# Scan stage of a hybrid SSD / attention layer: two elementwise steps per block formed by GpSimd instead of VectorE

## The chip, the cores and the metric

The kernel runs on one core of one Trainium2 chip, in one launch. The metric is the device time of that core in microseconds. The core has five engines with queues of their own: TensorE (PE in the profile; PEld is its weight load), VectorE (DVE), ScalarE (ACT), GpSimd (POOL) and SyncE (SP, which here issues DMAs). They wait for each other through semaphores only.

## The reference, cut to what matters

The model has two layers. Each layer mixes tokens by two groups of heads, a bidirectional state-space scan (SSD) and a latent attention, and then runs a feed-forward part (dense in layer 0, routed experts in layer 1). There are 512 latent tokens and 128 context tokens, that is five blocks of 128 tokens, which the scan treats as chunks. What the change touches is the scan's output:

```python
decay = jnp.exp(jnp.where(lower, seg, -jnp.inf))
scores = jnp.einsum('bcthn,bcshn->bctsh', cc, bc) * decay * dtc[:, :, None, :, :]
y_intra = jnp.einsum('bctsh,bcshp->bcthp', scores, xc)
...
y_inter = jnp.einsum('bcthn,bchpn->bcthp', cc, h_start) * jnp.exp(la)[..., None]
...
y_ssd = y_f + flip(y_b) + d_skip[:, None] * xs
y_ssd = y_ssd * jax.nn.silu(z)
```

The forward and the backward scan share B, C and x inside a chunk, so their decay matrices (each with its dt folded in) can be added first and multiplied by the shared C.B scores once.

## The kernel before, in words

`Mixer.run` calls, once per layer, `stage_in_proj`, `stage_ssd`, `stage_attention` and `stage_out_proj`. Each stage is one block of code per engine; all engines meet at a barrier at its end. Nothing reorders instructions: each engine runs the list that its function writes, and waits where the code says so.

`stage_in_proj` matters here for what its trace shows. GpSimd subtracts a rounded weight piece from the raw one (`split_lo`, L621, two inputs in SBUF, 128x2048 or 128x2752 elements), while VectorE runs the convolution (L737 and L739) on tiles in SBUF and copies results out of PSUM (L728 to L731).

`stage_ssd` first prepares (state, chunk states, the C.B scores `cbs`), then runs a loop over five blocks b = 0 to 4, the last of them the context. In the loop, with the lines of the profile:

- TensorE, block b: the inter-chunk product (L994, not for b = 4), then the decay exponents of block b+1 for both directions (L947, L949: `every_la`), then steps of the modulation matrix product that rides along (`mod`: L204 turns a finished row, L216 multiplies the next unit; a unit's L216 waits until VectorE has taken the unit before it), then y (L1007: scores times x, 16 records per block), which waits for the scores and for VectorE to be done with the y of the block before, and then the block's remaining modulation steps. After y of block 4 come the last unit (L216) and its turning.
- ScalarE, block b: the exponentials of block b+1 (L878: eight per direction, written to `seg`, which has two rooms, so it waits for y of block b-1), the copy of the modulation row (L242), and squares of the latents (L901, L903).
- VectorE, block b: adds the two directions' decays in place (L1114, 128x1024: the sum), multiplies by `cbs` (L1118: the multiply, which releases y on TensorE), forms d_skip times x (L1119, 128x512: the skip product, into t3), scales the inter-chunk product out of PSUM (L1124, twice), adds it up (L1127, L1128), takes a finished modulation unit (L232 out of PSUM, L234 from two SBUF tiles; L234 releases the next L216), waits for y, adds it (L1132) and multiplies by z (L1133, which counts `y_used`). In block 0 a second unit is taken (L232, L234) after L1133. In block 4 VectorE first waits for all squares (L1111, L1112).
- GpSimd has no code in this stage.

The stage ends with the last unit: L216, the row on ScalarE (L242), its turning, L232 and L234, and a reciprocal (L1138). SyncE loads the modulation weights ahead through eight rooms; these DMAs are idle in the last microseconds of the stage.

Of the kernel before, what the change touches and what calls it, by code (L numbers as in the profile page):

```python
# [16 lines left out]
ALU = mybir.AluOpType  # L17
# [3 lines left out]
P = 128  # L21
# [5 lines left out]
TB = T // P  # L27
LB = LAT // P
HT = T // 2
SEQ_OF = [0] * LB + [1]  # L30
SSDW, NH, HD, NG, NS = 512, 8, 64, 2, 64
# [47 lines left out]
def insert_dim(ap, at, n):  # L79

    dims = [list(d) for d in ap.ap]
    dims.insert(at, [0, n])
    return bass.AP(tensor=ap.tensor, offset=ap.offset, ap=dims)


class Program:
# [36 lines left out]
    def sb(self, name, shape, dt=F32, ctx=None):  # L123
        return (ctx or self.ctx).enter_context(self.nc.sbuf_tensor(name, shape, dt))
# [25 lines left out]
def chained(signal):  # L150

    count = [0]

    def link(eng, ins):
        count[0] += 1
        ins.then_inc(*signal.up())
        eng.wait_ge(*signal.at(count[0]))
    return link
# [594 lines left out]
def stage_ssd(p, l, t):  # L753

    nc, io = p.nc, p.io
    small, st_in = p.sig("ssd_small_ahead"), p.sig("ssd_state_ahead")
# [6 lines left out]
    st_turned, st_kept, turned, xst_dve, xst_act, btok_out = (p.sig(n) for n in (  # L763
        "ssd_st_turned", "ssd_st_kept", "ssd_turned", "ssd_xst_dve", "ssd_xst_act", "ssd_btok_out"))
# [4 lines left out]
    lab_ps, dec_ready, s_ready, inter_ps, inter_used, y_ps, y_used = (p.sig(n) for n in (  # L769
        "ssd_lab_ps", "ssd_decay", "ssd_scores", "ssd_inter_ps", "ssd_inter_used", "ssd_y_ps", "ssd_y_used"))  # L770
    squares, parts_ready = p.sig("pn_squares"), p.sig("silu_parts_ready")
    ahead_in, lat_mean, lat_root = p.sig("at_ahead_in"), p.sig("at_mean"), p.sig("at_root")
    with ExitStack() as own:
        def sb(name, shape):
            return p.sb(f"ssd_{name}{l}", shape, ctx=own)
# [24 lines left out]
        junk, junk2 = sb("junk", [P, QR]), sb("junk2", [P, KVR])  # L800
        cbs = sb("cbs", [P, NG, TB, P])
        t1, t2, t3 = sb("t1", [P, SSDW]), sb("t2", [P, SSDW]), sb("t3", [P, SSDW])
        seg = t["qkv_room"][:, 0:4 * NH * P].rearrange("p (r d h c) -> p r d h c", r=2, d=2, h=NH)
        xbc, z, xst, y = t["xbc"], t["z"], t["xst"], t["y_ssd"]
        dtb, alog, dsk, stl = t["dt_bias"], t["a_log"], t["d_skip"], t["stl"]
# [4 lines left out]
        act_blocks = (1, 2, 4)  # L810
# [3 lines left out]
        def mod_steps(slot):  # L814

            return [UNIT_STEPS * int(item[1]) + s for item in plan[slot]
                    for s in (range(MM_STEPS) if item[0] == "m" else (MM_STEPS,))]
# [5 lines left out]
        def by_block(tile):  # L823
            return tile.rearrange("p d b h -> p b d h")

        with nc.Block() as block:
            @block.sync
            def _(sp):
                mod.load(sp)
                sp.dma_start(t["past"], io["cache_ckv"][0, l]).then_inc(*ahead_in.up(16))  # L830
                sp.dma_start(t["kvrow"], io["kv_norm"][l].partition_broadcast(P)).then_inc(*ahead_in.up(16))
                sp.dma_start(t["cos"], io["rope_cos"].rearrange("(b p) r -> p b r", p=P)).then_inc(*ahead_in.up(16))
                sp.dma_start(t["sin"], io["rope_sin"].rearrange("(b p) r -> p b r", p=P)).then_inc(*ahead_in.up(16))
                sp.wait_ge(*fin_out.at(1))
                for d in range(2):
                    for g in range(2):
                        sp.dma_start(io["new_ssm"][0, l, d, 4 * g:4 * g + 4].rearrange("(j h) q n -> (h q) j n", h=2),
                                     stl[:, d, :, g * NS:(g + 1) * NS]).then_inc(*fin_stored.up(16))
                sp.wait_ge(*fin_stored.at(64))
# [174 lines left out]
            def _(dve):  # L1014
                link = chained(dve_c)
# [81 lines left out]
                def by_group(ap):  # L1097
                    return ap.rearrange("p (g h q) -> p g h q", g=NG, q=HD)

                def inter(d):  # L1100
                    return p.psum[:, 5:7, d * 256:(d + 1) * 256].rearrange("p g (h q) -> p g h q", q=HD)

                def heads(ap):
                    return ap.rearrange("p (h q) -> p h q", h=NH)
                dve.wait_ge(*scanned.at(1))
                for b in range(TB):
                    f, r = seg[:, b % 2, 0], seg[:, b % 2, 1]
                    if b == TB - 1:
                        dve.wait_ge(*squares.at(2 * TB))
                        stat = t["stat"]  # L1110
                        dve.tensor_scalar(stat[:, 0], stat[:, 0], 1.0 / QR, EPS, ALU.mult, ALU.add)  # L1111
                        dve.tensor_scalar(stat[:, 1], stat[:, 1], 1.0 / KVR, EPS, ALU.mult, ALU.add).then_inc(*lat_mean.up())  # L1112
                    dve.wait_ge(*dec_ready.at(2 * b + 2))
                    link(dve, dve.tensor_tensor(f, f, r, ALU.add))  # L1114
                    if b == 0:
                        dve.wait_ge(*cb_kept.at(1))
                    grouped = f.rearrange("p (g h) c -> p g h c", g=NG)
                    dve.tensor_tensor(grouped, grouped, insert_dim(cbs[:, :, b], 2, NH // NG), ALU.mult).then_inc(*s_ready.up())  # L1118
                    link(dve, dve.tensor_tensor(heads(t3[:]), heads(xst[:, b]), dsk[:].to_broadcast([P, NH, HD]), ALU.mult))  # L1119
                    if b < LB:  # L1120
                        dve.wait_ge(*inter_ps.at(b + 1))
                        for d, out in enumerate((t1, t2)):
                            grown = el[:, d, b].rearrange("p (g h) -> p g h", g=NG).to_broadcast([P, NG, NH // NG, HD])
                            ins = dve.tensor_tensor(by_group(out[:]), inter(d), grown, ALU.mult)  # L1124
                        ins.then_inc(*inter_used.up())
                        dve.wait_ge(*inter_used.at(b + 1))
                        link(dve, dve.tensor_tensor(t1[:], t1[:], t2[:], ALU.add))  # L1127
                        link(dve, dve.tensor_tensor(t3[:], t3[:], t1[:], ALU.add))  # L1128
                    for step in mod_steps(2 * b):
                        mod.on_vector(dve, step)  # L1130
                    dve.wait_ge(*y_ps.at(b + 1))
                    link(dve, dve.tensor_tensor(t3[:], t3[:], p.psum[:, 4], ALU.add))  # L1132
                    dve.tensor_tensor(y[:, b], t3[:], z[:, b], ALU.mult).then_inc(*y_used.up())  # L1133
                    dve.wait_ge(*y_used.at(b + 1))
                    for step in mod_steps(2 * b + 1):
                        mod.on_vector(dve, step)
# [1865 lines left out]
class Mixer:  # L3002
# [31 lines left out]
    def run(self, h, slots, ahead, r=None):  # L3034
        p, l, t = self.p, self.l, self.t
        p.silu_wide = t["silu_wide"]
        stage_in_proj(p, l, self.weights, h[:, 0], h[:, 1], t)
        self.inner.close()
        stage_ssd(p, l, t)
        self.scan.close()  # L3040
        stage_attention(p, l, t, slots)
        self.last = stage_out_proj(p, l, t, h, ahead, r)
        self.mixer.close()
# [146 lines left out]
```

## Time and profile before

| | us |
|---|---|
| median of 3 runs | 2041.09 (2039.52 to 2041.40) |
| span of the profiled execution, first to last instruction | 2035.5 |
| scan loop, layer 0 (first L1114 to the end of the last L1133) | 187.40 to 232.36 |
| scan loop, layer 1 (first L1114 to the end of the last L1133) | 1081.86 to 1126.96 |
| GpSimd busy, whole span | 98.2 in 64 instructions |
| VectorE busy, whole span | 1296.3 |

The profiled execution has no separate whole time in the list of times: what is known of it is its span, which is 5.6 us under the median. In the timeline a row gives start, length, engine, line, operation, the tile written <- the tiles read, the form, the count, and in brackets how long the engine stood idle before it and what ended that. A row with a count over one merges neighbours of the same line, and its length runs from the first start to the last end.

### The profile page before, as it was taken

The page shows a single profiled execution, that of the slowest core. Times are in us where ns is not written, and L with a number is a line of the kernel's source. Part 1 is how long each engine was busy: PE and PEld are TensorE (multiplying, and loading weights), DVE is VectorE, ACT ScalarE, POOL GpSimd, SP SyncE. Part 2 cuts the span into 40 slices and gives each one's busy share as a digit, 9 for nine tenths or more (in the row PEclk, how much of TensorE's full clock was granted, in tenths as well). Part 3 has the DMA queues.
Part 4 walks back from the last instruction along what each step waited for, and adds up shares of the span by engine and source line. Part 5 has one row for each costly group of instructions (what it writes and reads, how often), then busy time and mean ns, then how long its engine had stood idle before and what let it go on. Part 6 is the DMA issues. An engine that isn't in the chain of part 4 may idle for free. (4 is left out here: it accounts for less than half of the span.)

```text
span 2035.5 us, 31746 instructions
## 1 busy us (share of the span) xinstructions
PE 1909.9 (94%) x11144; PEld 1615.2 (79%) x11144; DVE 1296.3 (64%) x1973; ACT 1087.1 (53%) x1785; POOL 98.2 (5%) x64
## 2 busy tenths in 40 slices
PE   5997799899999999998988899889999999999998
PEld 2995575599998998997985665887888888888885
DVE  3835766574323333356817666657888888888888
ACT  4225654454211211235226554547888888888885
POOL 0330000000000000000400000002000000000002
PEclk9999899899999999998999899899999999999999
DMA  6204512202223213212216601149978191918395
GB/s 261 98 27 176 209 69 104 102 3 84 68 84 98 73 55 94 81 52 90 76 72 230 255 22 42 64 153 383 410 283 321 60 358 43 362 60 322 109 324 188
DMA packets 132849, 303.41 MB, mean 149 GB/s; under 512 B 20496, under 2 KB 66448, under 8 KB 129680
## 3 DMA queue, kind: packets, MB, share of 16 engines
q1 hardware_dynamic: 126608, 279.51, 37.9%
q10 hardware_dynamic: 3264, 12.07, 1.5%
q0 software_dynamic: 2880, 10.49, 1.4%
q8 instruction: 67, 1.10, 0.2%
q14 instruction: 30, 0.25, 0.0%
HBM read 360.43 MB, written 28.10 MB: 191 GB/s over the span
## 5 line engine op out<-in xcount | busy, mean ns | idle before, releaser
L2587 DVE TENSOR_TENSOR ex_wl<-ex_raw,ex_wh 128x1024 fp32r<-128x1024 f32 x351 | 418.8, 1220 | 25.6 <-ACT ex_wh L2426 14.3
L2426 ACT ACTIVATE ex_wh<-ex_raw 128x1024 fp32r<-128x1024 f32 x351 | 367.8, 1060 | 71.1 <-PE psum L2506 45.2
L2832 PE MATMUL psum<-norm_out,ex_w_hi 128*128 128x320 f32 x1408 | 267.7, 308 | 2.6 <-PEq L1771 2.6
L2506 PE MATMUL psum<-ex_wh,ex_he_hi 128*128 128x512 f32 (+1 forms) x624 | 242.2, 388 | 2.4 <-DVE ex_he_lo L2559 1.2
L2506 PE MATMUL psum<-ex_wl,ex_he_hi 128*128 128x512 f32 (+1 forms) x624 | 233.2, 374 | 0.1
L2506 PE MATMUL psum<-ex_wh,ex_he_lo 128*128 128x512 f32 (+1 forms) x624 | 232.9, 373 | 0.0
L2832 PEld LDWEIGHTS psum<-norm_out,ex_w_hi 128*128 128x128 f32 x1408 | 222.0, 187 | 3.0 <-DVE ex_w_lo L2693 2.8
L2693 DVE TENSOR_TENSOR ex_w_lo<-side,ex_w_hi 128x1024 fp32r<-128x1024 f32 (+1 forms) x82 | 82.6, 1014 | 166.3 <-ACT ex_w_hi L2689 166.0
L2832 PE MATMUL psum<-norm_out,ex_w_lo 128*128 128x320 f32 x704 | 165.2, 308 | 0.0
L2767 ACT ACTIVATE ex_sg_hf<-psum 128x640 f32<-128x640 f32 x22 | 15.5, 706 | 235.4 <-PE psum L2832 235.4
L2506 PEld LDWEIGHTS psum<-ex_wh,ex_he_hi 128*128 128x128 f32 x624 | 117.9, 189 | 25.0 <-issue 6.3
L2506 PEld LDWEIGHTS psum<-ex_wh,ex_he_lo 128*128 128x128 f32 x624 | 118.2, 189 | 22.2 <-issue 3.2
L2506 PEld LDWEIGHTS psum<-ex_wl,ex_he_hi 128*128 128x128 f32 x624 | 118.0, 189 | 20.9
L708 PE MATMUL psum<-win_hi,norm_out 128*128 128x256 f32 (+1 forms) x640 | 133.1, 300 | 0.1
L2689 ACT ACTIVATE ex_w_hi<-side 128x1024 fp32r<-128x1024 f32 (+1 forms) x82 | 70.5, 888 | 98.6 <-DMA side<-ffn_w_down 61.5
L2832 PEld LDWEIGHTS psum<-norm_out,ex_w_lo 128*128 128x128 f32 x704 | 118.7, 187 | 0.0
L708 PEld LDWEIGHTS psum<-win_hi,norm_out 128*128 128x128 f32 x640 | 104.7, 188 | 0.4 <-POOL win_lo L621 0.4
L2525 PE MATMUL psum<-ex_wh,ex_hh 128*128 128x512 f32 x260 | 104.7, 403 | 0.0
L2587 DVE TENSOR_TENSOR ex_wl<-x,ex_wh 128x1024 fp32r<-128x1024 f32 x65 | 77.2, 1220 | 38.6 <-ACT ex_wh L2426 38.6
L2525 PE MATMUL psum<-ex_wl,ex_hh 128*128 128x512 f32 x260 | 101.6, 391 | 0.0
L2525 PE MATMUL psum<-ex_wh,ex_hl 128*128 128x512 f32 x260 | 101.5, 390 | 0.0
L1513 PE MATMUL psum<-mx_qkv_room,at_qT 96*128 96x320 f32 (+3 forms) x320 | 92.6, 413 | 6.5 <-ACT at_items_room L1392 5.0
(462 smaller groups left out, 3903.7 us busy)
## 6 DMA issues: line engine op xcount, KB each, us to landing
ex_raw<-moe_gate_up SPq DMA_DIRECT2D x221, 512.0 KB
ex_raw<-moe_w_down SPq DMA_DIRECT2D x143, 512.0 KB
x<-moe_gate_up SPq DMA_DIRECT2D x64, 512.0 KB
wmod_ssd<-w_mod SPq DMA_DIRECT2D x56, 512.0 KB, 6.2
wmod_at<-w_mod SPq DMA_DIRECT2D x24, 512.0 KB, 4.1
side<-ffn_w_gate SPq DMA_DIRECT2D x22, 512.0 KB, 3.9
side<-ffn_w_up SPq DMA_DIRECT2D x22, 512.0 KB, 3.9
mx_qkv_room<-w_in SPq DMA_DIRECT2D x10, 1024.0 KB, 4.9
```

Of the source, the lines that this page charges most:

```text
L708: last = pe.matmul(p.psum[:, bank_of(g), 0:width], mh[:, k, j * P:(j + 1) * P], mw[:, k, :], start=(k == 0 and n == 0), stop=(k == KD - 1 ...
L1513: last = pe.matmul(p.psum[:, 2 * (n % 2) + part, 0:w], qT[0:rows, h, b * P:(b + 1) * P], kT[0:rows, h, lo + part * w:lo + (part + 1) * w], ...
L2426: act.activation(wh[:, i % RING], raw_of(i), ACT.Copy).then_inc(*hi_done.up(1))
L2506: last = pe.matmul(p.psum[:, 2 + g % 2, 0:width], h[:, k], w[:, i % RING, cols], start=(k == 0 and m == 0), stop=(k == KD - 1 and m == 2))
L2525: last = pe.matmul(p.psum[:, half], h[:, f], w[:, i % RING, cols], start=(f == 0 and m == 0), stop=False)
L2587: dve.tensor_tensor(wl[:, i % RING], raw_of(i), wh[:, i % RING].bitcast(F32), ALU.subtract).then_inc(*lo_done.up(1))
L2689: act.activation(self.wh[:, i % self.RING, part], self.room[:, i % 2, part], ACT.Copy).then_inc(self.hi_done, 1)
L2693: dve.tensor_tensor(self.wl[:, i % self.RING, part], self.room[:, i % 2, part], self.wh[:, i % self.RING, part].bitcast(F32), ALU.subtract ...
L2767: act.activation(sg.rearrange("p (a c) -> p a c", a=2), halves_of(home[i]), ACT.Silu).then_inc(*gate_act.up())
L2832: last = pe.matmul(p.psum[:, home[i] + half, 0:HT], m[:, i % w.RING, cols], x[:, k, half * HT:(half + 1) * HT], start=(k == 0 and n == 0), ...
```

## The change

The code of the scan's loop is split over two engines. GpSimd gets a function in this stage: per block it forms the skip product into a new tile `skip` with two rooms (d_skip times x, 128x512) and then, when the exponentials of both directions are there, the sum in place (128x1024). Its first skip product stands before the loop; the product of block b+1 stands in its list directly behind the sum of block b, and from block 2 on it waits until VectorE has finished the block two before. VectorE loses L1114 and L1119; its multiply waits for GpSimd's sum (`both_summed`), and its L1128 reads `skip`. Besides, the semaphores of the input projection are given back for reuse before the scan.

```diff
         t1, t2, t3 = sb("t1", [P, SSDW]), sb("t2", [P, SSDW]), sb("t3", [P, SSDW])
+        skip = sb("skip", [P, 2, SSDW])
...
+            @block.gpsimd
+            def _(pool):
+                pool.wait_ge(*small.at(0))
+                pool.wait_ge(*xst_dve.at(2))
+                pool.wait_ge(*xst_act.at(len(act_blocks)))
+                for b in range(TB):
+                    if b >= 2:
+                        pool.wait_ge(*y_used.at(b - 1))
+                    pool.tensor_tensor(heads(skip[:, b % 2]), heads(xst[:, b]), dsk[:].to_broadcast([P, NH, HD]),
+                                       ALU.mult).then_inc(*skip_ready.up())
+                    pool.wait_ge(*dec_ready.at(2 * b + 2))
+                    pool.tensor_tensor(seg[:, b % 2, 0], seg[:, b % 2, 0], seg[:, b % 2, 1],
+                                       ALU.add).then_inc(*both_summed.up())
...
-                    dve.wait_ge(*dec_ready.at(2 * b + 2))
-                    link(dve, dve.tensor_tensor(f, f, r, ALU.add))
+                    dve.wait_ge(*both_summed.at(b + 1))
...
-                    link(dve, dve.tensor_tensor(heads(t3[:]), heads(xst[:, b]), dsk[:].to_broadcast([P, NH, HD]), ALU.mult))
...
-                        link(dve, dve.tensor_tensor(t3[:], t3[:], t1[:], ALU.add))
+                        dve.wait_ge(*skip_ready.at(b + 1))
+                        link(dve, dve.tensor_tensor(t3[:], skip[:, b % 2], t1[:], ALU.add))
...
-                    link(dve, dve.tensor_tensor(t3[:], t3[:], p.psum[:, 4], ALU.add))
+                    if b == LB:
+                        dve.wait_ge(*skip_ready.at(b + 1))
+                    link(dve, dve.tensor_tensor(t3[:], t3[:] if b < LB else skip[:, b % 2], p.psum[:, 4], ALU.add))
...
+        for prefix in ("win_", "conv_"):
+            p.retire(prefix)
```

On VectorE, block 0 of the loop in layer 0 before (`mx_qkv_room` is `seg`, `halves` is x or y, `modsums` the modulation unit):

```order
L1114 TENSOR_TENSOR mx_qkv_room0<-mx_qkv_room0 128x1024 [waits ssd_decay,ssd_scanned]
L1118 TENSOR_TENSOR mx_qkv_room0<-mx_qkv_room0,ssd_cbs0 128x1024 [waits ssd_cb_kept,dve_chain]
L1119 TENSOR_TENSOR ssd_t30<-halves,mx_d_skip0 128x512
L1124 TENSOR_TENSOR ssd_t10<-psum,ssd_ect0 128x512 [waits ssd_inter_ps,dve_chain]
L1124 TENSOR_TENSOR ssd_t20<-psum,ssd_ect0 128x512
L1127 TENSOR_TENSOR ssd_t10<-ssd_t10,ssd_t20 128x512 [waits ssd_inter_used]
L1128 TENSOR_TENSOR ssd_t30<-ssd_t30,ssd_t10 128x512 [waits dve_chain]
L232 TENSOR_REDUCE modsums_ssd0<-psum 128x8 [waits mod_turned,dve_chain]
L234 TENSOR_TENSOR mod<-modsums_ssd0,vectors_sb 128x8 [waits mod_summed]
L1132 TENSOR_TENSOR ssd_t30<-ssd_t30,psum 128x512 [waits ssd_y_ps]
L1133 TENSOR_TENSOR halves<-ssd_t30,halves 128x512 [waits dve_chain]
```

The same place after the change, whose line numbers are those of the changed file:

```order
L1134 TENSOR_TENSOR mx_qkv_room0<-mx_qkv_room0,ssd_cbs0 128x1024 [waits ssd_cb_kept,ssd_both_summed,ssd_scanned]
L1139 TENSOR_TENSOR ssd_t10<-psum,ssd_ect0 128x512 [waits ssd_inter_ps]
L1139 TENSOR_TENSOR ssd_t20<-psum,ssd_ect0 128x512
L1142 TENSOR_TENSOR ssd_t10<-ssd_t10,ssd_t20 128x512 [waits ssd_inter_used]
L1144 TENSOR_TENSOR ssd_t30<-ssd_skip0,ssd_t10 128x512 [waits ssd_skip,dve_chain]
L232 TENSOR_REDUCE modsums_ssd0<-psum 128x8 [waits mod_turned,dve_chain]
L234 TENSOR_TENSOR mod<-modsums_ssd0,vectors_sb 128x8 [waits mod_summed]
L1150 TENSOR_TENSOR ssd_t30<-ssd_t30,psum 128x512 [waits ssd_y_ps]
L1151 TENSOR_TENSOR halves<-ssd_t30,halves 128x512 [waits dve_chain]
```

The sum and the skip product are gone from VectorE's list, the multiply stands first and waits for `ssd_both_summed`, and the second addition waits for `ssd_skip`; all else keeps its place.

On GpSimd, from the last weight pieces of the input projection of layer 0 to the attention stage, before:

```order
L621 TENSOR_TENSOR win_lo0<-mx_qkv_room0,win_hi0 128x2752 [waits win_hi_done] x2
L621 TENSOR_TENSOR win_lo0<-mx_qkv_room0,win_hi0 128x2048 [waits win_hi_done] x2
L650 UNCONDITIONAL_BRANCH
L1276 UNCONDITIONAL_BRANCH [waits barrier_Pool_Activation_PE_DVE_SP_gather]
L1278 MEMSET at_krt0 128x576
```

The same place after the change:

```order
L650 UNCONDITIONAL_BRANCH
L832 UNCONDITIONAL_BRANCH [waits barrier_Pool_Activation_PE_DVE_SP_gather]
L840 TENSOR_TENSOR ssd_skip0<-halves,mx_d_skip0 128x512 [waits ssd_xst_act,ssd_xst_dve,pool_chain]
L843 TENSOR_TENSOR mx_qkv_room0<-mx_qkv_room0 128x1024 [waits ssd_decay]
L840 TENSOR_TENSOR ssd_skip0<-halves,mx_d_skip0 128x512
L843 TENSOR_TENSOR mx_qkv_room0<-mx_qkv_room0 128x1024 [waits ssd_decay]
L840 TENSOR_TENSOR ssd_skip0<-halves,mx_d_skip0 128x512 [waits ssd_y_used]
L843 TENSOR_TENSOR mx_qkv_room0<-mx_qkv_room0 128x1024 [waits ssd_decay]
...
L831 UNCONDITIONAL_BRANCH
```

Ten instructions per layer stand there that were not there; the second skip product follows the first sum without any wait, the later ones wait for `ssd_y_used`.

## Rows read from the trace of the kernel before

**Rows 1.** The page, its first line.

```profile
span 2035.5 us, 31746 instructions
```

**Rows 2.** Timeline of VectorE in the scan of layer 0.

```profile
187.40 1.23 DVE L1114 TENSOR_TENSOR mx_qkv_room<-mx_qkv_room 128x1024 f32<-128x1024 f32 x1 [2.87 <-ACT mx_qkv_room L878]
188.66 1.22 DVE L1118 TENSOR_TENSOR mx_qkv_room<-mx_qkv_room,ssd_cbs 128x1024 f32<-128x1024 f32 x1
189.80 0.68 DVE L1119 TENSOR_TENSOR ssd_t<-halves,mx_d_skip 128x512 f32<-128x512 f32 x1
...
192.57 0.69 DVE L1128 TENSOR_TENSOR ssd_t<-ssd_t 128x512 f32<-128x512 f32 x1
...
193.52 0.17 DVE L234 TENSOR_TENSOR mod<-modsums_ssd,vectors_sb 128x8 f32<-128x8 f32 x1
...
199.30 0.17 DVE L234 TENSOR_TENSOR mod<-modsums_ssd,vectors_sb 128x8 f32<-128x8 f32 x1
...
209.49 1.22 DVE L1118 TENSOR_TENSOR mx_qkv_room<-mx_qkv_room,ssd_cbs 128x1024 f32<-128x1024 f32 x1
...
214.35 0.17 DVE L234 TENSOR_TENSOR mod<-modsums_ssd,vectors_sb 128x8 f32<-128x8 f32 x1
...
225.80 0.17 DVE L1111 TENSOR_SCALAR mx_stat<-mx_stat 128x5 f32<-128x5 f32 x1 [2.32 <-ACT ssd_junk L903]
...
227.20 1.22 DVE L1118 TENSOR_TENSOR mx_qkv_room<-mx_qkv_room,ssd_cbs 128x1024 f32<-128x1024 f32 x1
```

**Rows 3.** Timeline of TensorE in the scan of layer 0.

```profile
193.74 1.92 PE L216 MATMUL psum<-wmod_ssd,silu_wide 128*32 128x512 f32 x16 [2.33 <-DVE mod L234]
...
204.85 1.90 PE L1007 MATMUL psum<-halves,mx_qkv_room 128*128 128x64 f32 x16
...
228.48 2.43 PE L1007 MATMUL psum<-halves,mx_qkv_room 128*128 128x64 f32 x16 [2.97 <-DVE mx_qkv_room L1118]
230.84 3.12 PE L216 MATMUL psum<-wmod_ssd,silu_wide 128*32 128x512 f32 x16
```

**Rows 4.** Timeline of ScalarE in the scan of layer 0.

```profile
185.13 2.17 ACT L878 ACTIVATE mx_qkv_room<-psum,ssd_bias 128x128 f32<-128x128 f32 x8
...
190.08 4.23 ACT L878 ACTIVATE mx_qkv_room<-psum,ssd_bias 128x128 f32<-128x128 f32 x16 [1.60 <-PE psum L949]
...
203.74 4.23 ACT L878 ACTIVATE mx_qkv_room<-psum,ssd_bias 128x128 f32<-128x128 f32 x16 [1.63 <-PE psum L949]
```

**Rows 5.** Timeline of GpSimd in the input projection of layer 0.

```profile
74.56 4.60 POOL L621 TENSOR_TENSOR win_lo<-mx_qkv_room,win_hi 128x2048 fp32r<-128x2048 f32 x1 [6.99 <-ACT win_hi L617]
...
105.50 6.70 POOL L621 TENSOR_TENSOR win_lo<-mx_qkv_room,win_hi 128x2752 fp32r<-128x2752 f32 x1 [9.37 <-ACT win_hi L617]
```

**Rows 6.** Timeline of VectorE in the same stretch, in two narrow windows.

```profile
74.56 5.28 DVE L739 SCALAR_TENSOR_TENSOR conv_acc<-conv_pad,vectors_sb,conv_acc 128x644 f32<-128x644 f32 x1
...
105.31 7.58 DVE L739 SCALAR_TENSOR_TENSOR conv_acc<-conv_pad,vectors_sb,conv_acc 128x644 f32<-128x644 f32 x2
```

**Rows 7.** Line L739: count, then shortest, median and longest duration in ns.

```profile
L739 DVE SCALAR_TENSOR_TENSOR conv_acc<-conv_pad,vectors_sb,conv_acc x48: 887/890/6656, 68.0 to 1000.7; 128x644 f32<-128x644 f32 x48
```

**Rows 8.** Groups of GpSimd by form: busy us, mean ns of one, idle before.

```profile
L621 POOL TENSOR_TENSOR win_lo<-mx_qkv_room,win_hi 128x2048 fp32r<-128x2048 f32 x8 | 36.8, 4603 | 56.6 <-ACT win_hi L617 56.6
...
L2054 POOL TENSOR_TENSOR rt_strict<-tri,ident 128x128 f32<-128x128 f32 x1 | 0.5, 453 | 0.0
```

**Rows 9.** Timeline of GpSimd at the start: two neighbours without a wait.

```profile
2.15 0.28 POOL L302 TENSOR_SCALAR_AFFINE_SELECT tri<-tri 128x128 f32<-128x128 f32 x1
2.40 0.28 POOL L304 TENSOR_SCALAR_AFFINE_SELECT tri<-tri 128x128 f32<-128x128 f32 x1
```

**Rows 10.** Windows: start:end, length, busy us (x instructions) per engine, PEclk, DMA share, GB/s.

```profile
231.00:234.00 3.00, 2.96 (x16) 0.44 (x12) 1.33 (x2) 0.00 (x0) 0.00 (x0) 0.62 0.00 0
```

**Rows 11.** Timeline of VectorE, first sum in the scan of layer 1.

```profile
1081.86 1.22 DVE L1114 TENSOR_TENSOR mx_qkv_room<-mx_qkv_room 128x1024 f32<-128x1024 f32 x1 [2.87 <-ACT mx_qkv_room L878]
```

More of the change, by code:

```diff
@@ L771, in stage_ssd @@
     squares, parts_ready = p.sig("pn_squares"), p.sig("silu_parts_ready")
+    both_summed, skip_ready = p.sig("ssd_both_summed"), p.sig("ssd_skip")
     ahead_in, lat_mean, lat_root = p.sig("at_ahead_in"), p.sig("at_mean"), p.sig("at_root")
@@ L824, in by_block, with heads @@
             return tile.rearrange("p d b h -> p b d h")
+        def heads(ap):
+            return ap.rearrange("p (h q) -> p h q", h=NH)
         with nc.Block() as block:
+            @block.gpsimd
[11 more added lines that the diff above has]
+                                       ALU.add).then_inc(*both_summed.up())
             @block.sync
@@ L1101, in inter @@
                     return p.psum[:, 5:7, d * 256:(d + 1) * 256].rearrange("p g (h q) -> p g h q", q=HD)
-                def heads(ap):
-                    return ap.rearrange("p (h q) -> p h q", h=NH)
                 dve.wait_ge(*scanned.at(1))
                 for b in range(TB):
-                    f, r = seg[:, b % 2, 0], seg[:, b % 2, 1]
+                    f = seg[:, b % 2, 0]
                     if b == TB - 1:
```

## The prediction

> **What bounds the kernel now.** I read the page first, then the timelines of VectorE, TensorE and ScalarE over the scan of layer 0, and then those of GpSimd and VectorE over the input projection, because only there does the trace show GpSimd at elementwise work. The span is 2035.5 us [rows 1]; the change touches two loops of some 45 us each. The loop of layer 1 begins with the same 2.87 us of idle time before the same sum [rows 2, 11], so I work out layer 0 and count it twice.
>
> In the loop three engines hand work round. The first sum starts when ScalarE's exponentials end (185.13 + 2.17 = 187.30, sum at 187.40) [rows 2, 4]; the multiply follows, then VectorE works down to L234 at 193.52 to 193.69, and only then does TensorE's next unit start, at 193.74, after 2.33 us of idle time that L234 ended [rows 2, 3]. Behind that unit stand y of block 0, the next inter-chunk product and the exponents of block 2. So L234 sets the pace, and all that stands ahead of it on VectorE counts. In block 4 it is otherwise: VectorE waits for the squares until 225.80, its multiply ends at 227.20 + 1.22 = 228.42, and TensorE, 2.97 us idle, starts y(4) at 228.48 [rows 2, 3]. From there the last unit, its row and its turning follow in a line to the barrier, so **the start of y(4) is the quantity to work out**: what it moves by, the end moves by. Later stages load their data only once they are reached, so nothing absorbs it.
>
> **What the change removes.** Per block one sum of 1.23 us and one skip product of 0.68 us on VectorE [rows 2], 1.9 us with no cover on any block but the last. If that were all, 5 x 1.9 x 2 = 19 us would be at stake.
>
> **What it adds, and the price.** Five sums and five skip products per layer on GpSimd, of a form that the trace does not have. The nearest rows: 2048 columns with two inputs take 4603 ns, 128 columns 453 ns [rows 8]. The line through both has 176 ns at the root and 2.16 ns per column: 2.39 us for the sum (1024 columns) and 1.28 us for the skip product (512). Bounds: 2.30 and 1.15 us (a half and a quarter of 4603), and 3.62 and 1.81 us (eight and four times 453). I take the line, as the sizes lie between its ends. GpSimd starts about 0.08 us behind ScalarE's signal.
>
> **The lock.** Rows 5 and 6 show the two engines at work together, and they do not work side by side. At 74.56 GpSimd's subtraction and one of VectorE's L739 (two inputs in SBUF) start together; GpSimd ends at 79.16 after its usual 4.60 us, while L739, 0.89 us by its median [rows 7], takes 5.28 and ends at 79.84. At 105.31 an L739 has begun when GpSimd starts at 105.50 and runs through; the next one then ends at 105.31 + 7.58 = 112.89, against 112.20 for GpSimd [rows 5, 6], and that is the 6656 ns of [rows 7]. So whoever begins first keeps the other out, and a VectorE operation kept out ends at GpSimd's end plus its own length less 0.2 us. Hence in the loop L1118, L1127, L1128, L1133 and L234 (two SBUF inputs) are exposed. L1124, L1132 and L232 read PSUM, which no row shows beside such work; I take them as free, and were they held too, the walk below would end within 0.1 us of the same, since a sum or a skip product then only falls in front of them instead of the next operation.
>
> **The walk.** Block 0: sum 187.38 to 189.77 on GpSimd. Its second skip product needs no wait and stands right behind; neighbours on GpSimd start 0.03 us before the one in front ends (2.15 + 0.28 against 2.40) [rows 9], VectorE's multiply some 0.04 us after it. So the product holds the lock until 191.05 and the multiply ends at 192.07 instead of 189.88: 2.2 late. The skip product is no longer on VectorE: L1128 ends at 194.76 instead of 193.26, 1.5 late. Meanwhile the exponentials of block 1 are done (190.08 + 4.23 = 194.31) [rows 4] and the second sum takes the lock at 194.76 for about 2.2 us, in front of L234: 196.95 instead of 193.69, **3.2 late**, and with it the next unit, y(0) and L1133. `y_used` then releases the third skip product, and 1.28 us of it stand in front of the second L234: from 199.47 to 203.56, **4.1 late**.
>
> Block 1 adds nothing: its sum is long done, and VectorE is saved 1.9 us but waits for TensorE. The exponentials of block 2 end 4.1 late, at 203.74 + 4.23 + 4.1 = 212.0 [rows 4].
>
> Block 2: GpSimd sums from 212.05 to 214.44 with VectorE idle, the skip product behind it runs to 215.72, and the multiply ends at 216.74 instead of 209.49 + 1.22 = 210.71 [rows 2]: 6.0 late. The sum of block 3 again falls in front of L234 (219.4 to 221.6): 221.6 instead of 214.52, **7.1 late**. TensorE and ScalarE carry that to the exponentials of block 4.
>
> Block 4: these end at 230.0, the sum at 232.5. VectorE, already past the squares, multiplies until 234.0 instead of 228.42. Here the change gives back 1.5 us, because before, the sum stood behind the wait for the squares. **y(4) starts 5.5 us late**; with the lower prices of GpSimd 4.9, with the upper 12.6.
>
> By the Trainium skill, page "SBUF — State Buffer", section "SBUF: two separate sides", a VectorE operation with two SBUF inputs and a GpSimd operation that reads SBUF shut each other out of a shared pair of ports for the whole instruction, and the first to start gets it. Rows 5 and 6 agree on the whole instruction (5.28 us for a 0.89 us operation). By that rule the skip product behind a sum wins against the multiply, and y(4) is 5.5 us late; without any lock the same walk gives 0.9 us early (a rival below).
>
> **TensorE's clock.** After 2.33 us of idle time the unit at 193.74 runs its 1.92 us; after the 2.97 us before y(4) the granted clock falls, to a mean of 0.62 at 231 to 234 (mostly the 1.2 GHz level, where 1.00 is 2.4 GHz), and y and the unit take 2.43 and 3.12 us instead of 1.90 and 1.92: 1.7 us [rows 3, 10]. In the walk TensorE is idle from 191.3 to 197.0, 5.6 us: the same price in block 0. Before the unit of block 2 it is idle for 2.9 us, which may or may not do it (half of 1.7). Before y(4) it waits only 1.9 us, which may save the 1.7 paid today. I take +1.0 per layer, bounds -1.7 and +5.
>
> Giving semaphores back issues nothing. The first skip product of each layer starts at about 173.4, when x has been turned, and can hold VectorE for 1.3 us there; VectorE is idle for more than that, 2.87 us, before the loop [rows 2], which hides it. If it did not, 1.3 us a layer.
>
> **Sum.** 2 x (5.5 + 1.0) = 13.0 us on a span of 2035.5, so 2048.5. The median is 2041.1, 5.6 over the span, for what lies around it: **2054 us**. Its own range: from 2 x (4.9 - 1.7) = 6.4 to about 2 x (5.5 + 5) = 21, that is 2047.5 to 2062.
>
> **Rivals.**
> 1. The multiply wins the lock from the skip product (it decides by some 0.07 us). Then the multiply ends 1.04 us sooner in block 0 and L1128 is done before the second sum starts, so L234 is not held there either; the same walk gives y(4) 0.2 us late, and if y(4)'s wait no longer lowers the clock, 1.5 early. Time 2038 to 2043, here 2041: no change. For it: nothing in the trace shows this pair of operations. Against: the tie at 74.56 went to GpSimd.
> 2. No mutual hold in this loop, because the operations are shorter or of another form than L621. Then block 0 is 0.5 late (GpSimd's sum is 1.16 longer, the skip product 0.68 shorter), the middle blocks keep that, and block 4 gains the 1.26 us of the sum that stood behind the squares: y(4) 0.9 early, with the clock 2.6 early, 2 x 2.6: 2036. This is the other side, and it decides from the point that an L1128 or L234 beside a GpSimd sum keeps its 0.69 or 0.17 us. Against it stand rows 5 to 7: L739 is long held by every subtraction that it meets.
> 3. GpSimd is slower at these forms (a broadcast input, three dimensions), at the upper bounds: 12.6 per layer and the clock, 2 x 13.6, so 2068.
>
> **Chances.** Forecast 0.66, rival 1 0.16, rival 2 0.09, rival 3 0.09. A measurement of this kernel tells 0.2%, 4.1 us, from no change. Faster is rival 2: 0.09. Same is rival 1: 0.16. Slower is the rest: 0.75. The range leaves out rival 2 and most of rival 3 and takes in rival 1 and the forecast's own range: 2041 to 2062.
>
> **What would show it.** Right: in the timeline after, L234 of block 0 (and of block 2) lasts near 2 us; the multiplies of blocks 0 and 2 last near 2.2 us and end about 1 us after a skip product; y(4) starts some 5 us later after the first sum than the 41.1 us of today; PEclk falls in block 0. Wrong: L234 at 0.17 us beside a running GpSimd sum (rival 2), multiplies of 1.22 us directly behind the sum with the skip product stretched (rival 1), GpSimd sums well over 2.6 us (rival 3). The forecast also fails if GpSimd's list stalls before the loop, which shows as a first multiply later than 192.1.

## The result and the profile after

| | before | after |
|---|---|---|
| median, us (4 runs each) | 2040.82 (2039.52 to 2041.40) | 2060.93 (2058.59 to 2064.48) |
| ratio, with its 95% interval | | 1.0103 (1.0090 to 1.0116) |
| span of the profiled execution, us | 2035.5 | 2059.6 |
| mean granted TensorE clock, whole span | 0.976 | 0.966 |
| y(4), us after the first exponentials' end, layer 0 / 1 | 41.2 / 41.2 | 52.7 / 55.0 |

The changed kernel is 20.1 us slower; the forecast was 13 us slower, 2054, with the range 2041 to 2062. The mechanism was right; one term of the sum, the clock, was put too small.

The first line of the page after answers to [rows 1].

```profile
span 2059.6 us, 31785 instructions
```

This profiled execution took 2061.34 us, so 1.7 us lie around a span, not the 5.6 of the prediction. In 12 executions of before that were run later beside an experiment it was 1.7 to 1.8 as well (2040.67 us with a span of 2038.9, for one). The profiled execution of before, with its span of 2035.5, was thus some 3.6 us under its kernel's median of 2040.82, and the spans differ by 24.1 us where the medians differ by 20.1.

This is GpSimd in the scan of layer 0 (timeline: start, length, engine, line, operation, tiles, form, count, idle before and what ended it). In the changed file L843 is the sum and L840 the skip product.

```profile
185.75 2.36 POOL L843 TENSOR_TENSOR mx_qkv_room<-mx_qkv_room 128x1024 f32<-128x1024 f32 x1 [12.76 <-ACT mx_qkv_room L897]
188.07 1.04 POOL L840 TENSOR_TENSOR ssd_skip<-halves,mx_d_skip 128x512 f32<-128x512 f32 x1
192.76 2.34 POOL L843 TENSOR_TENSOR mx_qkv_room<-mx_qkv_room 128x1024 f32<-128x1024 f32 x1 [3.66 <-ACT mx_qkv_room L897]
203.95 1.04 POOL L840 TENSOR_TENSOR ssd_skip<-halves,mx_d_skip 128x512 f32<-128x512 f32 x1 [8.85 <-DVE halves L1151]
...
222.09 2.34 POOL L843 TENSOR_TENSOR mx_qkv_room<-mx_qkv_room 128x1024 f32<-128x1024 f32 x1 [3.77 <-ACT mx_qkv_room L897]
225.85 2.08 POOL L840 TENSOR_TENSOR ssd_skip<-halves,mx_d_skip 128x512 f32<-128x512 f32 x1 [1.43 <-DVE halves L1151]
```

This is VectorE in the same stretch, answering to [rows 2]: L1134 is the multiply (L1118 before), L1144 the second addition (L1128 before), L1128 the wait for the squares (L1111 before).

```profile
188.20 2.00 DVE L1134 TENSOR_TENSOR mx_qkv_room<-mx_qkv_room,ssd_cbs 128x1024 f32<-128x1024 f32 x1 [5.29 <-POOL mx_qkv_room L843]
...
192.15 0.69 DVE L1144 TENSOR_TENSOR ssd_t<-ssd_skip,ssd_t 128x512 f32<-128x512 f32 x1
192.88 0.19 DVE L232 TENSOR_REDUCE modsums_ssd<-psum 128x8 f32<-128x32 f32 x1
193.10 2.02 DVE L234 TENSOR_TENSOR mod<-modsums_ssd,vectors_sb 128x8 f32<-128x8 f32 x1
...
204.13 0.88 DVE L234 TENSOR_TENSOR mod<-modsums_ssd,vectors_sb 128x8 f32<-128x8 f32 x1
...
217.42 1.98 DVE L1134 TENSOR_TENSOR mx_qkv_room<-mx_qkv_room,ssd_cbs 128x1024 f32<-128x1024 f32 x1 [2.34 <-POOL mx_qkv_room L843]
...
222.31 2.14 DVE L234 TENSOR_TENSOR mod<-modsums_ssd,vectors_sb 128x8 f32<-128x8 f32 x1
...
225.81 1.22 DVE L1134 TENSOR_TENSOR mx_qkv_room<-mx_qkv_room,ssd_cbs 128x1024 f32<-128x1024 f32 x1
...
236.99 0.17 DVE L1128 TENSOR_SCALAR mx_stat<-mx_stat 128x5 f32<-128x5 f32 x1 [2.17 <-ACT ssd_junk L922]
237.07 0.16 DVE L1129 TENSOR_SCALAR mx_stat<-mx_stat 128x5 f32<-128x5 f32 x1
237.14 1.22 DVE L1134 TENSOR_TENSOR mx_qkv_room<-mx_qkv_room,ssd_cbs 128x1024 f32<-128x1024 f32 x1
```

Read the two fences together. The skip product (188.07) stands in GpSimd's list behind the sum, so it starts 0.13 us ahead of the multiply, which lasts 2.00 instead of 1.22 us. The second sum starts at 192.76, while VectorE is at L1144; L232, with its input in PSUM, runs through beside it (0.19), but L234, with two small SBUF inputs, waits for the sum's end: 2.02 instead of 0.17 us. Both repeat in block 2, and the third skip product holds the second L234 (0.88). At 225.81 it is the other way round: the multiply began 0.04 us before the skip product, and GpSimd is held (2.08 instead of 1.04).

The next fence is TensorE, answering to [rows 3], with units (L216) and y (L1026) of blocks 0, 2 and 4. ScalarE's first exponentials, answering to [rows 4], end at 183.50 + 2.17 = 185.67.

```profile
195.18 3.64 PE L216 MATMUL psum<-wmod_ssd,silu_wide 128*32 128x512 f32 x16 [5.39 <-DVE mod L234]
198.75 3.68 PE L1026 MATMUL psum<-halves,mx_qkv_room 128*128 128x64 f32 x16
...
205.07 3.26 PE L216 MATMUL psum<-wmod_ssd,silu_wide 128*32 128x512 f32 x16 [1.79 <-DVE mod L234]
...
224.51 3.32 PE L216 MATMUL psum<-wmod_ssd,silu_wide 128*32 128x512 f32 x16 [3.06 <-DVE mod L234]
...
238.41 3.58 PE L1026 MATMUL psum<-halves,mx_qkv_room 128*128 128x64 f32 x16 [1.72 <-DVE mx_qkv_room L1134]
241.93 3.61 PE L216 MATMUL psum<-wmod_ssd,silu_wide 128*32 128x512 f32 x16
```

```profile
183.50 2.17 ACT L897 ACTIVATE mx_qkv_room<-psum,ssd_bias 128x128 f32<-128x128 f32 x8
```

The windows answer to [rows 10]; the third figure from the right is the granted clock (1.00 is 2.4 GHz, 0.50 is 1.2 GHz). First the loop after, then two windows of the loop before.

```profile
186.00:190.00 4.00, 3.78 (x22) 2.62 (x20) 1.80 (x1) 2.40 (x9) 3.11 (x2) 1.00 0.97 366
190.00:195.00 5.00, 0.00 (x0) 0.00 (x0) 4.86 (x7) 2.69 (x11) 2.24 (x1) 0.92 0.29 119
195.00:199.00 4.00, 3.82 (x17) 0.84 (x18) 0.12 (x1) 0.12 (x1) 0.10 (x1) 0.50 0.19 54
...
203.00:206.00 3.00, 1.21 (x10) 0.28 (x12) 2.90 (x5) 0.00 (x0) 1.04 (x1) 0.50 0.42 172
206.00:209.00 3.00, 3.00 (x22) 1.01 (x16) 0.15 (x1) 0.59 (x1) 0.00 (x0) 0.70 0.31 106
```

```profile
190.00:194.00 4.00, 1.67 (x13) 1.10 (x15) 3.51 (x7) 3.92 (x16) 0.00 (x0) 1.00 0.79 301
...
226.00:229.00 3.00, 0.52 (x5) 0.52 (x5) 2.97 (x4) 0.00 (x0) 0.00 (x0) 1.00 0.01 3
```

TensorE is idle from 190 to 195, and from 195 the clock is at the 1.2 GHz level for over ten microseconds: unit, y, the next wait and the second unit all lie in it. In the loop before, the windows from 186 to 229 all have 1.00, and only its end ran at the lower level [rows 10].

### The profile page after: what moved, and what is told of

Read it like the earlier page. It is cut to its first block and busy times, and to the rows that moved or that the text cites. A ratio compares the mean times of both kernels' runs of the same rounds, so it can differ in the third digit from the quotient of the medians.

```text
span 2059.6 us, 31785 instructions
## 1 busy us (share of the span) xinstructions
PE 1925.6 (93%) x11144; PEld 1620.9 (79%) x11144; DVE 1291.7 (63%) x1953; ACT 1086.7 (53%) x1785; POOL 132.7 (6%) x84
```

## The experiments

All times are medians; ratios are against runs of before on the same chip (2040.08 us for experiments 1 to 4, 2039.63 for 5 to 8, 2040.97 for 9 and 10). "y(4)" is the start of the y of block 4 after the end of the first exponentials, layer 0 / layer 1.

**1. The sum alone on GpSimd** (VectorE keeps the skip product).

```diff
-pool.tensor_tensor(heads(skip[:, b % 2]), heads(xst[:, b]), ...)
+link(dve, dve.tensor_tensor(heads(t3[:]), heads(xst[:, b]), ...))   # behind the multiply
```

> Only the sum stays on GpSimd; the skip product is back on VectorE behind the multiply. Theory A (the two engines shut each other out, and TensorE's clock falls after the long waits that follow): the second sum still takes the lock in front of L234 in block 0, and the fourth in block 2, some 2 us each; TensorE stands idle 5.4 and 3.6 us there, y(4) starts 4.3 us late per layer before the clock counts, and the clock costs as much as in the changed kernel: 2057 to 2062 us. Theory B (GpSimd's sum is only slower and lies in series, no lock): y(4) 0.4 us late per layer, 2040 to 2045 us, L234 at 0.17 us throughout.

It took 2061.37 us, ratio 1.0103 (1.0084 to 1.0123), with y(4) at 52.8 / 52.1: the whole loss is there without the skip product. These are GpSimd's second sum and VectorE's L234 (timeline):

```profile
192.95 2.34 POOL L837 TENSOR_TENSOR mx_qkv_room<-mx_qkv_room 128x1024 f32<-128x1024 f32 x1 [4.58 <-ACT mx_qkv_room L891]
```

```profile
193.32 1.99 DVE L234 TENSOR_TENSOR mod<-modsums_ssd,vectors_sb 128x8 f32<-128x8 f32 x1
```

L234 comes 0.37 us behind the sum's start and is held to its end.

**2. The skip product alone on GpSimd.**

```diff
-pool.tensor_tensor(seg[:, b % 2, 0], seg[:, b % 2, 0], seg[:, b % 2, 1], ALU.add)
+link(dve, dve.tensor_tensor(f, f, r, ALU.add))
```

> Only the skip product stays on GpSimd; the sum is back on VectorE. Theory A: products of 1.04 us hold L234 in block 0 and the multiplies of blocks 2 and 3 for some 0.6 us each, which eats what VectorE is spared: y(4) 0.3 us early per layer, TensorE's waits as in the kernel before, 2038 to 2042 us. Theory B: nothing is held, y(4) 1.8 us early per layer, 2035 to 2038 us.

It took 2041.78 us, 1.0006 (0.9996 to 1.0015), with y(4) at 42.7 / 42.5. The time is in theory A's range, but y(4) is not: it was expected 0.3 us early and came 1.5 and 1.3 us late. The second L234 is held as expected (0.88 us); the unit behind it waits 2.21 us and, in both layers, runs at the lower clock (3.46 us in layer 0), which the expectation left out. In the trace the 0.68 us per block less on VectorE do not pay for that; the medians show no difference.

**3. Both on GpSimd, the skip products ahead of need** (four rooms; none stands behind a sum in the loop, and block 4's stays on VectorE).

```diff
+for b in (0, 1): product(b)
+pool.wait_ge(*scanned.at(1))
+for b in (2, 3): product(b)
 for b in range(TB):
-    pool.tensor_tensor(heads(skip[:, b % 2]), ...)
     pool.wait_ge(*dec_ready.at(2 * b + 2))
     pool.tensor_tensor(seg[:, b % 2, 0], ...)
```

> The sum stays on GpSimd, and its skip products of blocks 0 to 3 are made ahead of the loop, two of them after the chunk states are done; that of block 4 is on VectorE. Theory A: nothing stands between sum and multiply, L1128 and L234 of block 0 are done some 0.2 us before the second sum starts, so neither is held; y(4) is 0.8 us early per layer and TensorE's longest wait is 2.8 us: 2037 to 2041 us, or about 2049 if the clock falls already after 2.8 us. If the place of the skip product does not matter (the sum is what costs): 2057 to 2062 us, as with the sum alone.

It took 2037.36 us, 0.9987 (0.9978 to 0.9997), with y(4) at 40.7 / 42.0. In layer 0 all five sums are still on GpSimd, at 2.36 to 2.57 us. But now the multiply is not held, VectorE has no skip product in blocks 0 to 3, and L234 comes ahead of the second sum:

```profile
194.65 0.17 DVE L234 TENSOR_TENSOR mod<-modsums_ssd,vectors_sb 128x8 f32<-128x8 f32 x1
```

```profile
195.09 2.37 POOL L847 TENSOR_TENSOR mx_qkv_room<-mx_qkv_room 128x1024 f32<-128x1024 f32 x1 [4.67 <-ACT mx_qkv_room L901]
```

L234 starts some 0.4 us ahead of the sum here and 0.4 us behind it in experiment 1: with the same sums at the same price, **which of the two starts first goes with most of the 20 us**. How much the order alone is worth is not shown, since this kernel also frees VectorE of four skip products. A hold as such need not cost that much: in block 2 the fourth sum holds the multiply by z (L1155, 2.66 instead of 0.69 us), but L234 of that block had gone, and TensorE's unit was under way (216.03, after a wait of 1.00 us).

**4. TensorE kept busy in the first wait** (changed kernel, with 22 products in front of the first unit whose results nobody uses).

```diff
+pe.wait_ge(*fin_out.at(1))
+for _ in range(22): pe.matmul(p.psum[:, 4], p.ident_r[:], ...)
 mod.on_tensor(pe, step)   # the first unit
```

> The changed kernel, with 22 matmuls of 0.235 us into PSUM columns that are free at that point put into TensorE's wait for L234 in block 0; their results are not used. Theory A (the first unit, y(0) and the second unit are long because the clock fell during 5.4 idle us): they come back to about 1.9 us each from 3.64, 3.68 and 3.26, 4.8 us per layer: 2049 to 2054 us. Rival (they are long for another cause, such as waiting for weights or for VectorE inside): 2060 to 2062 us, with the three durations unchanged.

It took 2058.66 us, 1.0092 (1.0075 to 1.0109): a miss, less gain than expected. At the place itself it did what it should, with the unit at 1.92 and y(0) at 2.00 us. But the clock fell at the next wait instead:

```profile
195.21 1.92 PE L216 MATMUL psum<-wmod_ssd,silu_wide 128*32 128x512 f32 x16 [0.43 <-DVE mod L234]
197.07 2.00 PE L1030 MATMUL psum<-halves,mx_qkv_room 128*128 128x64 f32 x16
...
201.72 3.24 PE L216 MATMUL psum<-wmod_ssd,silu_wide 128*32 128x512 f32 x16 [2.21 <-DVE mod L234]
```

**5. The next unit released by L232** instead of by the held L234.

```diff
-pe.wait_ge(*self.taken.at(n - self.banks + 1))
+pe.wait_ge(*(self.summed if self.rows_by_scalar else self.taken).at(n - self.banks + 1))
```

> The changed kernel, but TensorE's next unit is released by L232, which has read the PSUM bank, instead of L234. Theory A (what the hold costs reaches TensorE mainly through L234): L234 is still held for 2 us, but the unit of block 0 starts after 3.4 instead of 5.4 idle us and that of block 2 without a long wait; y(4) is 0.2 us late per layer before the clock counts; the clock still falls once, in block 0, about 4 us: 2045 to 2052 us. Rival (the late multiplies set the loop, L234 does not matter): 2057 to 2062 us.

It took 2049.29 us, 1.0044 (1.0031 to 1.0058). L234 is still held (2.05 and 2.15 us), but with TensorE no longer behind it over half of the loss is gone. y(4) is at 45.6 where the clock fell (layer 0) and at 41.6 where it did not.

**6 and 7. Useless work on GpSimd beside the kernel before**: an addition of two tiles, or a memset, whose results nobody uses and nobody waits for, at the places of the sums.

```diff
+pool.wait_ge(*dec_ready.at(2 * b + 2))
+link(pool, pool.tensor_tensor(idle[:, 0], idle[:, 0], idle[:, 1], ALU.add))   # 6
+link(pool, pool.memset(idle[:], 0.0))                                        # 7, 128x2048
...
+for prefix in ("win_", "conv_"): p.retire(prefix)                            # both
```

> The kernel before, and beside it GpSimd adds two private tiles of 128x1024 each time both directions' exponentials of a block are there; nobody waits for the result and it is not used. VectorE does all of its work as before. Theory A (lock): the addition shuts out L1114 or L1118 in block 0 and L1128 and L1114 later for some 2 us each, TensorE's waits grow to 6.4 us in block 0 and 3.8 in block 2, y(4) is 7.9 us late per layer and the clock adds to it: 2060 to 2072 us. Theory B (only waiting for GpSimd's result costs): 2039 to 2042 us.

> The same as the additions beside, with a memset of 128x2048 (about 1.9 us) in the place of each addition, so that GpSimd is busy at the same places but reads nothing. If reading is what takes the lock: nothing of VectorE's is held, 2039 to 2042 us. If any GpSimd work does: 2 us holds as with the additions, 2055 to 2070 us.

The additions took 2067.98 us, 1.0127 (1.0096 to 1.0158), the memsets 2040.34 us, 1.0002 (0.9989 to 1.0015). With the additions, VectorE's multiply and its second addition end behind GpSimd's addition (1.22 and 0.69 us in [rows 2]):

```profile
186.91 3.42 POOL L834 TENSOR_TENSOR ssd_idle<-ssd_idle 128x1024 f32<-128x1024 f32 x1 [22.11 <-ACT mx_qkv_room L887]
193.93 2.34 POOL L834 TENSOR_TENSOR ssd_idle<-ssd_idle 128x1024 f32<-128x1024 f32 x1 [3.60 <-ACT mx_qkv_room L887]
```

```profile
188.12 3.29 DVE L1127 TENSOR_TENSOR mx_qkv_room<-mx_qkv_room,ssd_cbs 128x1024 f32<-128x1024 f32 x1
...
194.10 2.72 DVE L1137 TENSOR_TENSOR ssd_t<-ssd_t 128x512 f32<-128x512 f32 x1
```

With a memset beside them, the sum, which lies wholly inside it, and the multiply keep their times:

```profile
185.97 1.80 POOL L833 MEMSET ssd_idle<- 128x2048 f32 x1 [46.67 <-ACT mx_qkv_room L886]
```

```profile
186.02 1.23 DVE L1122 TENSOR_TENSOR mx_qkv_room<-mx_qkv_room 128x1024 f32<-128x1024 f32 x1 [2.87 <-ACT mx_qkv_room L886]
187.28 1.22 DVE L1126 TENSOR_TENSOR mx_qkv_room<-mx_qkv_room,ssd_cbs 128x1024 f32<-128x1024 f32 x1
```

Nobody waits for either result, so neither a wait for GpSimd nor its slower result is what costs. The addition reads SBUF and holds, the memset only writes it and does not. The Trainium skill, page "SBUF — State Buffer", section "Who interferes with whom", says so: a VectorE operation with two SBUF inputs contends with a GpSimd operation that reads SBUF, not with one that only writes. Experiments 6 and 7 agree, 28 us against none. Experiment 7 also gives the semaphores of the input projection back, so that part of the change costs nothing that shows.

**8. VectorE forms the products ahead of the loop** (kernel before; GpSimd does nothing here): those of blocks 0 to 3 in its 2.87 us of idle time before the first sum, the wait for the squares stands behind the last multiply, and in block 0 the unit is taken ahead of the two additions.

```diff
+for b in range(LB):
+    last = dve.tensor_tensor(heads(skip[:, b]), heads(xst[:, b]), ...)
...
-if b == TB - 1: dve.wait_ge(*squares.at(2 * TB)) ...   # before the sum
 ... multiply ...
+if b == TB - 1: dve.wait_ge(*squares.at(2 * TB)) ...
...
+if b == 0: for step in mod_steps(0): mod.on_vector(dve, step)
 ... two additions ...
```

> The kernel before without GpSimd in the scan: VectorE makes the skip products of blocks 0 to 3 ahead of the loop, where it is idle for 2.87 us; in block 4 it multiplies before it waits for the squares; in block 0 it takes the finished modulation unit (L232, L234) before the additions. Theory A (L234 in block 0, VectorE's own length in blocks 2 and 3 and the wait for the squares in block 4 set the loop): y(4) 5.5 us early per layer, and without the 3 us wait before it the clock does not fall there, 1.7 us more: 2025 to 2031 us. If VectorE does not set the loop: 2038 to 2042 us.

It took 2024.04 us, 0.9911 (0.9881 to 0.9942), with y(4) at 36.1 / 36.1: faster than both kernels, and 1 us under the range expected. How the gain divides over the three edits is not shown. y(4) waits only 0.70 us in both layers. In layer 0 the clock stays up behind that, in layer 1 (third row) it does not:

```profile
222.82 2.00 PE L1008 MATMUL psum<-halves,mx_qkv_room 128*128 128x64 f32 x16 [0.70 <-DVE mx_qkv_room L1117]
224.75 1.92 PE L216 MATMUL psum<-wmod_ssd,silu_wide 128*32 128x512 f32 x16
...
1112.42 2.76 PE L1008 MATMUL psum<-halves,mx_qkv_room 128*128 128x64 f32 x16 [0.70 <-DVE mx_qkv_room L1117]
```

**9. TensorE kept busy in all four waits** (experiment 4, and unused products in front of the second unit, block 2's unit and y(4) too).

```diff
+if b == LB: pe.wait_ge(*inter_used.at(LB)); fill(5, 7)             # before y(4)
+if b in (0, 2) and step % UNIT_STEPS == 0:                         # second unit, block 2's unit
+    pe.wait_ge(*inter_used.at(b + 1)); fill(5, 9 if b == 0 else 12)
```

> The changed kernel, with products whose results nobody uses put into TensorE's list at all four places where it waits longer than before: in front of the first unit (as in the kernel that filled this one wait alone), in front of the second unit, of block 2's unit and of y(4). Only TensorE's idle time goes; what VectorE and GpSimd do stays. Theory A (the walk's 4.9 us per layer are the waits, and the rest of the measured +11.5 and +13.8 us is the clock that falls after them): the units behind the filled waits keep 1.9 to 2.0 us, y(4) starts 45 to 48 us after the first exponentials (changed kernel 52.7 and 55.0, before 41.2), and the time is 2040 + 2 x 5 = 2050 us, 2046 to 2053. Theory B (the falls come from something else in the changed loop than TensorE's waiting): units and y(4) stay near 3.3 to 3.6 us, y(4) at 49 to 52, time 2055 to 2061.

It took 2045.34 us, 1.0019 (1.0009 to 1.0029), with y(4) at 46.5 / 46.5: theory A, 0.7 us under its range. VectorE and GpSimd still do all that they do in the changed kernel, the held L234 included (2.08 us), but the granted clock is 1.00 from 190 to 241, and four fifths of the loss are gone:

```profile
197.81 1.92 PE L216 MATMUL psum<-wmod_ssd,silu_wide 128*32 128x512 f32 x16 [0.43 <-DVE mod L234]
...
204.31 1.92 PE L216 MATMUL psum<-wmod_ssd,silu_wide 128*32 128x512 f32 x16
...
222.47 1.92 PE L216 MATMUL psum<-wmod_ssd,silu_wide 128*32 128x512 f32 x16 [0.32 <-DVE mod L234]
...
234.74 2.00 PE L1035 MATMUL psum<-halves,mx_qkv_room 128*128 128x64 f32 x16
236.67 1.92 PE L216 MATMUL psum<-wmod_ssd,silu_wide 128*32 128x512 f32 x16
```

My 2050 left out that y(4) and the last unit also run faster than before (3.92 us together instead of 5.55 [rows 3]).

**10. Experiments 8 and 5 together.**

> The kernel that beat both (VectorE forms the skip products ahead of the loop, the wait for the squares stands behind the last multiply, the first unit is taken ahead of the two additions of block 0), with one more edit: in the scan TensorE's next unit is released by the reduce out of PSUM (L232) instead of by L234. Theory A (each unit's release lies on the path, 0.2 us of L234 per unit, some of it covered): y(4) 0.3 to 1.0 us earlier per layer than 36.1, time 2021 to 2024 where that kernel has 2024.0. Theory B (in that kernel TensorE no longer waits for the unit in most blocks): no difference, 2023 to 2026.

It took 2022.52 us, 0.9913 (0.9897 to 0.9930), with y(4) at 35.7 / 35.7. The 0.4 us per layer show in the trace, but the ratio is that of experiment 8: these runs can't tell a difference.

## Why the prediction was right, and which term was too small

Experiment 9 runs the changed schedule with the clock up, so the walk (the prediction's order of waits, without the clock) can be held against it term by term (us later than before, layer 0, each counted from the end of the first exponentials):

| end of | forecast | clock kept up (9) | after |
|---|---|---|---|
| multiply, block 0 | 2.2 | 1.96 | 1.95 |
| second addition, block 0 (L1128 before) | 1.5 | 1.22 | 1.21 |
| first L234 | 3.2 | 3.13 | 3.06 |
| second L234 | 4.1 | 3.86 | 7.17 |
| multiply, block 2 | 6.0 | 5.65 | 10.32 |
| L234, block 2 | 7.1 | 6.96 | 11.56 |
| y(4), its start | 5.5 | 5.33 | 11.56 |

**The lock and the walk: right.** Each wait stands where it was put, and y(4) gets back about 1.5 us at the squares. The small differences are GpSimd's price: the sum took 2.36 us (estimate 2.39), the skip product 1.04 (estimate 1.28; it is even under the lower bound of 1.15), so its broadcast input costs nothing visible.

**The rivals.** Rival 1 (the multiply wins) is refuted in blocks 0 and 2; in block 3, where another signal releases the skip product, the multiply did win. Rival 2 (no hold) is refuted by L234 at 2.02 us, rival 3 (slow forms) by 1.04 and 2.36 us. The first skip product, ahead of the loop, holds two neighbours on VectorE there (2.04 instead of 1.29 us together), but VectorE's next wait for TensorE is shorter by as much (1.61 instead of 2.36 us), and it cost nothing: the first exponentials end 1.63 us earlier than before (185.67 against 187.30 [rows 4]), and 1.66 us lie already between the starts of layer 0's input projection (58.93 against 60.59).

**The clock: mis-sized.** The term that failed is "I take +1.0 per layer, bounds -1.7 and +5". In the profiled executions y(4) starts 52.7 - 46.5 = 6.2 us later than with the clock kept up in layer 0, and 8.5 us in layer 1. The end moved by more than y(4) did, against the prediction's "what it moves by, the end moves by": y(4) and the last unit themselves take 3.58 + 3.61 us in layer 0 and 2.99 + 3.64 in layer 1, against 3.92 with the clock up. Off go the 1.6 us per layer that before pays there too. That makes 7.9 and 9.6 us for the clock in the traces, above the bound of +5. By the medians, which hold the usual execution of before, it is (20.1 - 2 x 5.3) / 2 = 4.7 per layer.

That the time lies inside the range is thus partly luck. By the traces the two loops cost 2 x 5.3 + 7.9 + 9.6 = 28.1 us, over the range's top of 21 us. The spans differ by 4.0 us less, because the traced execution of the changed kernel was shorter outside the loops; among the twelve traces the stretches ahead of, between and behind the loops differ by 2.6 to 4.3 us. The medians differ by another 4.0 us less, chiefly because the traced execution of before was a quick one (3.6 us).

The step that failed is that I priced each fall at one unit and one y (1.7 us). The clock stayed low for over ten microseconds, through the following wait, and took the second unit with it; each such delay moved the next exponents, and the units of block 2 and y(4) fell again behind waits of 3.06 and 1.72 us. That y(4)'s shorter wait would save the 1.7 us did not come true either.

Two things stay open: which waits lower the clock and which do not (below), and how the 4.7 us per layer of the medians divide over the waits, since there is a trace of only one execution of each kernel.

## What to carry to other kernels

Before elementwise work with SBUF inputs is moved to GpSimd, look for VectorE's operations with two SBUF inputs that will meet it, tiny ones above all: an 8-column operation that releases TensorE can be held as long as the sum that it meets lasts (2.02 instead of 0.17 us), and less than half a microsecond of order can decide it. Price a longer TensorE wait with all that runs behind it at the lower clock, not with the next product alone. Where VectorE idles just ahead of a loop, try work there before moving it to another engine (experiment 8, where two more edits helped).

## What was not expected of the hardware

- The same wait lowers the clock in one place and not in another. In experiment 3 the first unit waits 2.78 us in both layers; it then takes 1.92 us in layer 0 and 3.26 in layer 1. In experiment 7 the second unit waits 1.49 us in both, and takes 3.47 and 1.92 us. In experiment 8 y(4) waits 0.70 us in both, and takes 2.00 and 2.76 us. The length of the wait alone thus does not tell whether the clock falls.
- The profiled execution of before had a mean clock of 0.976. The 49 executions of before beside the experiments had 0.970 to 0.977, at 2048.24 us for the one with 0.970 and at 2037.06 and 2037.58 us for the two with 0.977. One execution's clock thus goes with some microseconds.
- GpSimd is held as VectorE is, and 0.04 us of order decided it in block 3: the skip product there took 2.08 instead of 1.04 us.
